# Rotary embedding read from PSUM by VectorE, and the index selection one slab earlier, in a four-layer fp32 kernel

## What is computed

```python
def apply_partial_rope(t, cos, sin):          # first quarter of each head's dims
    x1, x2 = tf[..., :half], tf[..., half:]
    r = concatenate([x1 * c - x2 * s, x2 * c + x1 * s])
    return concatenate([r, t[..., rot:]])

q  = apply_partial_rope(q  (8 heads x 128), cos_a, sin_a)
k  = apply_partial_rope(k  (2 heads x 128), cos_a, sin_a)
qi = apply_partial_rope(qi (8 heads x 64),  cos_i, sin_i)
ki = apply_partial_rope(ki (1 head  x 64),  cos_i, sin_i)
rel   = relu(einsum('bqhd,bsd->bqhs', qi, ki))
score = einsum('bqhs,bqh->bqs', rel, wi)      # causal, else -inf
_, sel = top_k(score, 64)                     # per query
a = softmax(q k / sqrt(128), only over sel) v
```

## Time and profile before

| what | value |
|---|---|
| device time, median of 3 runs | 1864.31 us (1863.62 to 1864.72) |
| time of the profiled execution | 1862.73 us |
| its span | 1860.9 us |
| PE busy | 1764.1 us, 95% |
| DVE busy | 1352.6 us, 73% |
| ACT busy | 1003.7 us, 54% |
| POOL busy | 655.6 us, 35% |
| chain that ended last | PE 72%, DVE 19%, ACT 6%, issue 2% |
| granted PE clock, mean | 0.973 |

### The profile page before, as it was taken

One profiled execution on the slowest core, in us unless ns is written; L12 is line 12 of the kernel. 1 busy time (PEld: TensorE's weight loads), 2 busy tenths in 40 slices (PEclk: granted clock), 3 DMA queues, 4 the chain that ended last, 5 costly groups with the idle time before them and its releaser, 6 DMA issues.

```text
span 1860.9 us, 33510 instructions
## 1 busy us (share of the span) xinstructions
PE 1764.1 (95%) x13890; PEld 1699.9 (91%) x13890; DVE 1352.6 (73%) x1919; ACT 1003.7 (54%) x1528; POOL 655.6 (35%) x397
## 2 busy tenths in 40 slices
PE   6989999898999989999999999998999999999998
PEld 5989999886899989898889999998899988999997
DVE  3768765655686756996679689774898478859795
ACT  4465444473654544467564466444466556356462
POOL 5641104461310245344454411036334456341113
PEclk8999999898999989999999999998999999999999
DMA  7435645431455544454334455554345333545552
GB/s 263 141 101 181 203 163 170 158 120 51 134 186 187 174 150 146 136 182 148 101 118 167 161 170 189 184 184 140 119 162 185 118 112 128 177 151 189 198 168 83
DMA packets 80503, 288.27 MB, mean 155 GB/s; under 512 B 8928, under 2 KB 9184, under 8 KB 80224
## 3 DMA queue, kind: packets, MB, share of 16 engines
q1 hardware_dynamic: 79488, 283.15, 45.8%
q10 hardware_dynamic: 864, 2.98, 0.4%
HBM read 285.05 MB, written 1.05 MB: 154 GB/s over the span
## 4 chain that ended last, share of the span: by engine, by line
PE 72%; DVE 19%; ACT 6%; issue 2%; POOL 0%; DMA 0%; ACTq 0%; DVEq 0%; SPq 0%; POOLq 0%
PE lin L634 22%; PE lin L636 22%; PE lin L635 22%; DVE acc L1614 3%; DVE w_lo L451 3%; ACT w_hi L1105 2%; DVE arena L2053 1%; DVE sq L1994 1%; DVE sq L1526 1%; ACT sq L1468 1%; DVE arena L1881 1%; PE lin L906 1%; PE stat L701 1%; PE tr L1023 1%; PE logit L864 1%
## 5 line engine op out<-in xcount | busy, mean ns | idle before, releaser
L634 PE MATMUL lin<-h_hi,w_hi 128*128 128x256 f32 x2976 | 856.1, 288 | 15.4 <-DVE h_lo L460 8.6
L635 PE MATMUL lin<-h_lo,w_hi 128*128 128x256 f32 x2976 | 847.1, 285 | 0.0
L636 PE MATMUL lin<-h_hi,w_lo 128*128 128x256 f32 x2976 | 846.9, 285 | 0.0
L1105 ACT ACTIVATE w_hi<-w_raw 128x1024 fp32r<-128x1024 f32 (+1 forms) x546 | 537.0, 1031 | 379.1 <-PE lin L636 377.8
L451 POOL TENSOR_TENSOR w_lo<-w_raw,w_hi 128x1024 fp32r<-128x1024 f32 (+1 forms) x194 | 467.4, 2417 | 419.6 <-ACT w_hi L1105 414.0
L634 PEld LDWEIGHTS lin<-h_hi,w_hi 128*128 128x128 f32 x2976 | 576.8, 194 | 19.9 <-DVE h_lo L460 8.2
L635 PEld LDWEIGHTS lin<-h_lo,w_hi 128*128 128x128 f32 x2976 | 576.5, 194 | 2.2 <-issue 1.9
L636 PEld LDWEIGHTS lin<-h_hi,w_lo 128*128 128x128 f32 x2976 | 576.1, 194 | 0.0
L451 DVE TENSOR_TENSOR w_lo<-w_raw,w_hi 128x1024 fp32r<-128x1024 f32 (+1 forms) x352 | 491.1, 1399 | 48.4 <-ACT w_hi L1105 47.5
L634 PE MATMUL lin<-hid_hi,w_hi 128*128 128x256 f32 x912 | 260.6, 286 | 2.3 <-DVE hid_lo L460 2.3
L635 PE MATMUL lin<-hid_lo,w_hi 128*128 128x256 f32 x912 | 258.3, 283 | 0.0
(11 more groups left out here) (273 smaller groups left out, 2094.8 us busy)
## 6 DMA issues: line engine op xcount, KB each, us to landing
w_raw<-in_upA SPq DMA_DIRECT2D x112, 512.0 KB, 3.7
w_raw<-in_upB SPq DMA_DIRECT2D x64, 512.0 KB, 4.2
w_raw<-in_xbc SPq DMA_DIRECT2D x48, 512.0 KB, 4.3
w_raw<-in_dnA SPq DMA_DIRECT2D x32, 512.0 KB, 3.6
w_raw<-in_dnB SPq DMA_DIRECT2D x32, 512.0 KB, 3.6
w_raw<-in_z SPq DMA_DIRECT2D x32, 512.0 KB, 4.1
w_raw<-in_gates SPq DMA_DIRECT2D x32, 512.0 KB, 4.2
w_raw<-in_ps SPq DMA_DIRECT2D x32, 512.0 KB, 4.1
```

The lines of the kernel that those rows point to most:

```text
L634: nc.tensor.matmul(out, lhs[0], rhs[0], start=first, stop=False)
L635: nc.tensor.matmul(out, lhs[0], rhs[1], start=False, stop=False)
L636: return nc.tensor.matmul(out, lhs[1], rhs[0], start=False, stop=last)
L1105: nc.scalar.activation(w_hi[slab.slot][:, half, part], w_raw[slab.slot][:, half, part], ACT.Copy)\
```

## The change

The output channels of the projections for `q`, `k`, `qi` and `ki` are laid out anew (`rotary_rows`, `head_rows`, `index_rows`), so that the two rotated halves of a head stand 64 partitions apart. DVE then reads the slab's PSUM bank itself: one product with cos over 128 partitions, two products with sin over 64 partitions each, whose outputs go to the other 64 partitions of `stat` in PSUM, and the sum out of SBUF and PSUM. `swap` on PE and `raw_copy` on ACT are gone, and DVE frees the bank.

The index key stands in two chunks, `ki2` is 128x2x256: each chunk has the key in the rows of one of the two heads of a `qi` chunk and zeros elsewhere (by the tables `cos_ki`, `sin_ki`). The index products contract over 128 rows instead of 64. PE's index products come one slab earlier, and so do scores and selection on DVE.

```diff
         dil = arena[:, 69 * T:69 * T + NDIL]
 
...
-                def swap(which, n, stage, at=0):
-                    r = rope_unit[0]
-                    rope_unit[0] += 1
-                    slab_at(stage, at, l).wait_released(pe)
-                    if r >= 1:
-                        pe.wait_ge(s.rope_done, 8 * l + r)
-                    nc.tensor.matmul(stat[:, 0:n], const(which),
-                                     rope_raw[:, r % 2, :, :].rearrange("p c t -> p (c t)")[:, 0:n],
-                                     start=True, stop=True).then_inc(s.rope_rot, 1)
-
                 products("kidtwi", h_op, l, normed(4 + 2 * l))
 
...
-                    if b >= 1:
+                    if b == 0:
+                        pe.wait_ge(s.rope_done, 8 * l + 3)
+                    else:
                         pe.wait_ge(s.ix_rel, 4 * l + b)
                     for i in range(4):
                         head = 4 * half + i
-                        lo = 64 * (head % 2)
-
                         mm = nc.tensor.matmul(logit[:, 2 * (i % 2) + i // 2, 0:(t + 1) * P],
-                                              qi2[lo:lo + 64, head // 2, t * P:t * P + P],
-                                              ki2[lo:lo + 64, 0, 0:(t + 1) * P], start=True, stop=True)
+                                              qi2[:, head // 2, t * P:t * P + P],
+                                              ki2[:, head % 2, 0:(t + 1) * P], start=True, stop=True)
                     mm.then_inc(s.ix_mm, 1)
 
                 slab_products(slab_at("qi", 0, l), h_op)
-                swap("swap_idx", T, "kidtwi")
+                pe.wait_ge(s.rope_in, l + 1)
                 for t in range(2):
-                    mm = nc.tensor.transpose(tr[:, t * IH:(t + 1) * IH], dscr[SH:SH + IH, 2, t * P:t * P + P],
-                                             ident[SH:SH + IH, SH:SH + IH])
+                    mm = nc.tensor.transpose(tr[:, t * IH:(t + 1) * IH], dscr[WI_AT:WI_AT + IH, 2, t * P:t * P + P],
+                                             ident[WI_AT:WI_AT + IH, WI_AT:WI_AT + IH])
                 mm.then_inc(s.wi_tr, 1)
                 slab_products(slab_at("qi", 1, l), h_op)
-                swap("swap_idx", 2 * T, "qi", 0)
                 slab_products(slab_at("k", 0, l), h_op)
-                swap("swap_idx", 2 * T, "qi", 1)
+                index_products(0)
                 for n in range(4):
                     slab_products(slab_at("q", n, l), h_op)
-                    if n == 0:
-                        swap("swap_attn", 2 * T, "k")
-                    else:
-                        swap("swap_attn", 2 * T, "q", n - 1)
-                    index_products(n)
+                    if n < 3:
+                        index_products(n + 1)
                 slab_tokens(slab_at("v", 0, l))
...
-                rope_unit = [0]
-
-                def raw_copy(slab, chunks):
-
-                    r = rope_unit[0]
-                    rope_unit[0] += 1
-                    if r >= 2:
-                        act.wait_ge(s.rope_done, 8 * l + r - 1)
-                    return nc.scalar.activation(rope_raw[:, r % 2, 0:chunks, :], lin[slab.bank][:, 0:chunks, :], ACT.Copy)
-
...
                 nc.scalar.activation(small[0:SH, 40:41], pcol2(l, "a_log")[0:SH, :], ACT.Exp).then_inc(s.a_exp, 1)
                 act.wait_ge(s.dt_abs, l + 1)
                 nc.scalar.activation(dscr[0:SH, 3, :], dscr[0:SH, 3, :], ACT.Exp, scale=-1.0).then_inc(s.dt_e, 1)
-
-                def rope_copy(slab):
-                    done(slab)
-                    raw_copy(slab, 2).then_inc(s.bank_free[slab.bank], 1)
 
                 def rectified(b):
                     n = (b // 2 + 1) * P
                     act.wait_ge(s.ix_mm, 4 * l + b + 1)
                     nc.scalar.activation(ix_rel[:, b, :, 0:n], logit[:, :, 0:n], ACT.Relu).then_inc(s.ix_rel, 1)
 
-                rope_copy(slab_at("qi", 0, l))
+                done(slab_at("qi", 0, l))
                 act.wait_ge(s.wi_tr, l + 1)
                 nc.scalar.activation(small[:, 42:58], tr[:, 0:2 * IH], ACT.Copy).then_inc(s.wi_copied, 1)
-                rope_copy(slab_at("qi", 1, l))
-                rope_copy(slab_at("k", 0, l))
+                done(slab_at("qi", 1, l))
+                done(slab_at("k", 0, l))
                 for n in range(4):
-                    rope_copy(slab_at("q", n, l))
                     rectified(n)
+                    done(slab_at("q", n, l))
                 slab = slab_at("v", 0, l)
...
-                def rope(out, chunks, which):
-                    r = rope_unit[0]
+                def rope(out, slab, cos, sin):
+
+                    raw, part = lin[slab.bank], stat[:, :].rearrange("p (c t) -> p c t", t=T)
+                    slab.wait_done(dve)
+                    lower, upper = slice(0, P // 2), slice(P // 2, P)
+                    tt(out, raw[:, :, :], cos, ALU.mult)
+                    if rope_unit[0]:
+                        dve.wait_ge(s.rope_done, 8 * l + rope_unit[0])
                     rope_unit[0] += 1
-                    base = 8 * 2 * l + 2 * r
-                    raw, part = rope_raw[:, r % 2, 0:chunks, :], rope_t[:, 0, 0:chunks, :]
-                    cos, sin = (const(f"{f}_{which}", T).unsqueeze(1).to_broadcast([P, chunks, T])
-                                for f in ("cos", "sin"))
-                    dve.wait_ge(s.rope_rot, 8 * l + r + 1)
-                    tt(out, raw, cos, ALU.mult).then_inc(s.rope_chain, 1)
-                    tt(part, stat[:, 0:chunks * T].rearrange("p (c t) -> p c t", t=T), sin, ALU.mult)\
-                        .then_inc(s.rope_chain, 1)
-                    dve.wait_ge(s.rope_chain, base + 2)
+                    for to, of in ((lower, upper), (upper, lower)):
+                        ins = tt(part[to, :, :], raw[of, :, :], sin[of, :, :], ALU.mult)
+                    ins.then_inc(s.bank_free[slab.bank], 1)
+                    slab.wait_released(dve)
                     tt(out, out, part, ALU.add).then_inc(s.rope_done, 1)
+
+                def tables(which):
+                    return [const(f"{f}_{which}", T).unsqueeze(1).to_broadcast([P, 2, T]) for f in ("cos", "sin")]
 
                 dt, adt, cum = (dtb[0:SH, i, :] for i in range(3))
                 arg, mag = dscr[0:SH, 2, :], dscr[0:SH, 3, :]
-                slab_at("kidtwi", 0, l).wait_released(dve)
-                rope(ki2[:, :, :], 1, "idx")
+                rope(ki2[:, :, :], slab_at("kidtwi", 0, l),
+                     *[const(f"{f}_idx", 2 * T).rearrange("p (c t) -> p c t", t=T) for f in ("cos", "sin")])
                 ch = Chain(dve, s.dt_chain, DT_LINKS * l)
...
-                    rope(qi2[:, 2 * n:2 * n + 2, :], 2, "idx")
+                    rope(qi2[:, 2 * n:2 * n + 2, :], slab_at("qi", n, l), *tables("idx"))
                 take_over(dve, "k", 1, l)
                 weights(slab_at("k", 0, l))
-                rope(k2[:, :, :], 2, "attn")
-                weights(slab_at("q", 0, l))
+                rope(k2[:, :, :], slab_at("k", 0, l), *tables("attn"))
+                index_scores(0, 0)
                 rounds = TOPK // 8
                 for n in range(4):
-                    rope(q2[:, 2 * n:2 * n + 2, :], 2, "attn")
-                    weights(slab_at("q", n + 1, l) if n < 3 else slab_at("v", 0, l))
-                    if n < 2:
-                        index_scores(0, n)
+                    weights(slab_at("q", n, l))
+                    rope(q2[:, 2 * n:2 * n + 2, :], slab_at("q", n, l), *tables("attn"))
+                    if n == 0:
+                        index_scores(0, 1)
+                    elif n == 1:
+                        top_eights(0, range(0, rounds // 2))
                     elif n == 2:
-                        top_eights(0, range(0, rounds // 2))
-                    else:
                         top_eights(0, range(rounds // 2, rounds))
                         selection(0)
+                    else:
+                        index_scores(1, 0)
                     step_sizes(n)
+                weights(slab_at("v", 0, l))
+                index_scores(1, 1)
 
                 def da_mask(u):
...
-                    if n < 2:
-                        index_scores(1, n)
-                    elif n < 2 + rounds:
-                        top_eights(1, range(n - 2, n - 1))
-                    elif n == 2 + rounds:
+                    if n < rounds:
+                        top_eights(1, range(n, n + 1))
+                    elif n == rounds:
                         selection(1)
                     if n == 3:
                         da_mask(0)
                     if n == 7:
...
-        sin[0:half], sin[half:rot] = -np.sin(ang), np.sin(ang)
-        put(f"swap_{name}", np.kron(np.eye(heads), swap))
-        put(f"cos_{name}", np.tile(cos, (heads, 1)))
-        put(f"sin_{name}", np.tile(sin, (heads, 1)))
```

(32 more changed lines are left out.)

42 lines of the change are left out of this document (18 added, 24 removed).

## The result

| what | before | after |
|---|---|---|
| device time, median (runs) | 1863.96 us (1863.02 to 1864.72, 4) | 1844.1 us (1840.0 to 1847.14, 4) |
| ratio, 95% interval | | 0.9892 (0.9868 to 0.9916) |
| time of the profiled execution, span | 1862.73, 1860.9 us | 1840.0, 1838.0 us |
| PE, DVE busy | 1764.1, 1352.6 us | 1748.6, 1348.7 us |
| granted PE clock, mean | 0.973 | 0.981 |

The kernel is 1.1% faster, 19.9 us by the medians. The forecast was 1844. The stage row is taken from the timeline of PE, from the first product of `kidtwi` to the attention product `tr<-sq,arena` that follows `z` 0 (L1023 before, L1004 after).

What follows compares the result with a forecast made beforehand. PE bounds the start of the third layer's rotary stage and DVE falls behind in it. Per layer 6.45 - 2.4 + 0.34 + 3.4 + 2.65 - 1.2 = 9.2 us, twice 18.5, from 1862.73: 1844 us, range 1838 to 1850.

Steps and rivals of the forecast that it cites:

- Swaps, 6.45 us per layer: On PE: seven swaps of 512 columns at 0.86 us and one of half the width at 0.43 go, 6.45 us.
- Index products, -2.4 us: On PE: contracting over 128 rows makes the index products longer, 2 x 0.45 + 2 x 0.75 = 2.4 us per layer.
- Old pause and its clock, 6.05 us: PE's wait for half 1 of xbc 4: 3.4 us goes, with 2.65 us of half clock behind it.
- New pause, -1.2 us: PE waits 1.2 us for DVE's half 1 of xbc 1, no clock charged; bounds 0 and 4.2 us.
- Unit of 2.55 us: DVE's rotary unit becomes four instructions with one wait between, 2.55 us instead of 1.94.
- The rule of the Trainium skill that I had weighed and not taken: DVE's 64-partition products: changing partition group waits for earlier instructions; 2 us per layer in the new pause, 1847 to 1848.
- The other rule weighed there: DVE's PSUM operands: 120 fixed cycles against 58 for SBUF; DVE 1.6 us later, time 1847.
- the rival of an instruction twice as long: DVE's rotary units: reading and writing PSUM takes about 1.3 us per instruction, DVE bounds the stage, 1870 us; chance 0.05.
- Holding: DVE's rotary sums, lengthened beside POOL's subtraction: 7.9 us of this goes, as every new instruction has a PSUM operand.
- the 1 us charged: DVE before xbc 1: 1 us added for holding by POOL that comes back in other work with two SBUF inputs.
- The rival of the holding in full: POOL's holding of DVE all comes back: new pause 4.2 us with clock, 3.6 us gained per layer, 1855.5; chance 0.12.
- Later pause of 1.73 us: PE's pause at 841.3, hanging on ACT behind the last taps: left as it was, plus or minus 1.7 us.

Runs made afterwards that it cites:

- noswap: The kernel before without its swap products on PE, DVE's unit waiting for ACT's copy instead (rotary embedding not the reference's): 1851.3 us, ratio 0.9932.
- rows64: The changed kernel with index products contracting over 64 rows again (scores not the reference's): 1843.8 us, ratio 0.9892.
- late: The changed kernel with its rotary part alone; index products, scores, selection and xbc 1's subtraction in the order of before: 1850.16 us, ratio 0.9925.
- again: The changed kernel itself run once more, with no edit: 1845.34 us, ratio 0.9899; its profiled execution had a span of 1844.3 us.

## Why the prediction was right

Its mechanism held for what was removed, for what was added and for the place of the new pause; it left the later pause in place, which went. Several sizes were off, and they offset each other.

- **Swaps, 6.45 us per layer.** Right: "noswap" alone gains 12 us, with 1.7 us of it lost again in longer waits for its logits.
- **Index products, -2.4 us.** Too much. I took the difference of durations; from start to next start it is 0.81 against 0.64 (724.66 to 725.30) and 1.54 against 1.07 (739.56 to 740.63), 1.3 us; "rows64" has 1.04. The swap ahead of them, likewise, had held 0.95 us (723.71 to 724.66) instead of 0.86. The forecast for all that PE does before its logits was 4.4 us, and the two timelines have 5.9: 1.5 us per layer better.
- **Old pause and its clock, 6.05 us.** Gone in both layers. "late" shows that the rotary part alone does not do it (3.25 us left) and "noswap" that taking the swaps off PE does not (3.40 left); the order without the rotary part was not run. From the transposes behind `xbc` 2 to the logits behind `xbc` 11 PE gained 6.0 us in the third layer and 4.9 in the fourth: the forecast took the clock of the third layer, 2.65 us, for both, and the fourth had half of it.
- **New pause, -1.2 us.** Right place, 2.17 us. DVE's start was forecast at 760.9 and came at 759.60; PE wanted the half at 758.7 and not at 760.9. Of both, 0.8 us is the first block, which was that much shorter in this execution; the rest of PE's is the 1.5 us above. By "rows64" whatever PE saves before this point is added to the pause.
- **Unit of 2.55 us.** It takes 2.75. The rule of the Trainium skill that I had weighed and not taken ("VectorE: DVE Perf Modes", section "Two Vector instructions with no wait between them") is what the spacing shows: 0.69 us before the other 64 partitions against 0.60 without them. The other rule weighed there (the Trainium skill, same page, section "The TRN2 errata — SBUF-src ops pay a fixed extra latency per instruction"), a higher fixed cost of PSUM operands, is not borne out: 0.684, 0.700 and 0.686 us with PSUM against 0.69 out of SBUF. By that too the rival of an instruction twice as long fell.
- **Holding.** 7.9 us of it left the rotary units. The two holds of 2.38 us at 730 and 756 us are no return of it: the kernel before had two as well, one below and 2.37 us at 748.03. New are some 1.9 us before `w_lo` of `xbc` 1 (1.87 us for 1.22 at 712.21, two rows of scores 0.6 us longer each), about 1.3 us of them in front of a wait for PE, so the 1 us charged was fair. DVE's waits for slabs fell to 4.2 us, not 6.7. The rival of the holding in full was priced too low: 4.2 us of pause stand for 3.0 us more of holding, where the text says four and all of it would be 6.9.
- **Later pause of 1.73 us, left as it was.** Gone. It had its cause in DVE: before, the last taps ended at 840.1 behind an instruction held for 2.52 us (834.01), ACT's copy followed at 840.70 and PE at 841.33. That instruction is the last of the second half's selection, and one slab ahead the selection ends behind `xbc` 8 instead of `xbc` 10. The pause stays in "late" and "noswap", where it ends behind `xbc` 10, and is gone in the runs with the new order; no run moves this instruction alone.

The two held instructions of the kernel before, of the last two points:

```profile
740.34 2.28 DVE L1547 TENSOR_TENSOR sq<-sq,arena 32x256 f32<-32x256 f32 x1
...
834.01 2.52 DVE L1897 TENSOR_TENSOR arena<-arena,cst 128x256 f32<-128x256 f32 x1
```

Per layer 9.2 + 1.5 - 1.0 + 1.7 = 11.4 us; the two stages gave 11.5 and 11.7. For the third layer that is the account. In the fourth it is luck: its old clock was worth 1.3 us less than charged, and 1.3 us came from a shorter stretch of 0.50 at the beginning of its stage, which "again" does not have. That is the profiled execution at 1840.0. The four executions lie at 1840.0 and 1841.5 and at 1846.7 and 1847.1 us, and the median of 1844.1, which met the forecast, is the mean of the middle two. By "again" the longer ones pay clock behind the 2.2 us pause, a longer stretch of 0.50 at the beginning of the fourth layer's stage and more waiting in the first block. A charge for clock was left out of the forecast on one row of a pause without it; right for one execution, wrong for another.

## What to carry to other kernels

When an engine is freed of work, find the first place at which another engine's queue is now late; the gain ends there, and a further saving on the freed engine before it ("rows64") is worth nothing. Here that place is fixed by the order of the small instructions, so after a change of operations move the subtractions that the fastest engine waits for ahead of the work that nobody waits for: some 9 us more here, at no cost. Charge an instruction by start to next start, not by its duration.
